# Value-row gathers four pairs behind expert-row gathers in a streaming encoder step with product-key experts

## The reference, cut to what matters

```python
def one_block(xb):                       # up to 128 tokens
    q = (xb @ w_q).reshape(PEER_BLOCK, P_HEADS, 2, P_HALF)
    s = jnp.einsum('nhpe,hpke->nhpk', q, subkeys)
    top_s, top_i = lax.top_k(s, P_TOPK)  # 16 of 128 keys, in each half
    ...                                  # 256 sums, the best 16 per head: idx, (tokens, 8, 16)
    g = jax.nn.softmax(best_s, axis=-1)
    ue = u[idx]                          # rows of 1024 floats
    ve = v[idx]
    a = jax.nn.gelu(jnp.einsum('nd,nhkd->nhk', xb, ue))
    return jnp.einsum('nhk,nhkd->nd', g * a, ve)
```

## Time and profile before

| what | value |
|---|---|
| time, median of 3 runs | 4091.41 us (4071.89 to 4091.5) |
| span of the profiled execution | 4095.0 us |
| PE busy | 2611.7 us (64%) |
| DVE busy | 2381.8 us (58%) |
| POOL busy | 2496.3 us (61%) |
| DMA, mean over the span | 361 GB/s, 1478.18 MB |
| u and v gathers | 1152 and 1152, of 512 KB |
| first dot of stage 1 | 590.6 us after the span's start |

### The profile page before, as it was taken

How to read it: one execution, slowest core, us unless ns; L and a number is a source line. 1 busy time by engine, 2 the same in 40 slices (tenths; PEclk the granted TensorE clock), 3 DMA queues, 4 the chain that set the end, 5 groups by cost and what they waited for, 6 DMA issues and landing times.

```text
span 4095.0 us, 31715 instructions
## 1 busy us (share of the span) xinstructions
PE 2611.7 (64%) x9649; PEld 951.6 (23%) x9649; DVE 2381.8 (58%) x6038; ACT 459.4 (11%) x1098; POOL 2496.3 (61%) x2374
## 2 busy tenths in 40 slices
PE   7878664654564465546456675665555687767789
PEld 2344341221231111212112132222212221111122
DVE  2247687875666456645764565776566657754410
ACT  2234220111010000100010011011001100000000
POOL 1102446667777667665765565566667677777776
PEclk8889876777776686768677787867777799999999
DMA  8855888999999999989998998999899999999999
GB/s 340 304 182 162 303 275 301 353 343 360 371 397 372 364 409 384 383 335 407 405 400 326 400 391 305 389 380 355 337 409 407 361 403 409 405 410 409 409 409 374
DMA packets 480551, 1478.18 MB, mean 361 GB/s; under 512 B 59088, under 2 KB 132864, under 8 KB 479712
## 3 DMA queue, kind: packets, MB, share of 16 engines
q0 software_dynamic: 347792, 1268.25, 80.6%
q1 hardware_dynamic: 107008, 195.85, 13.1%
q10 hardware_dynamic: 25584, 12.06, 1.0%
HBM read 1448.97 MB, written 28.57 MB: 361 GB/s over the span
## 4 chain that ended last, share of the span: by engine, by line
DMA 36%; POOL 22%; PE 18%; DVE 13%; issue 9%; ACT 1%; SPq 0%; ACTq 0%; DVEq 0%; POOLq 0%
DMA A<-in_uv,A 34%; POOL A L2013 12%; POOL A L2033 10%; PE P L961 9%; DVE A L1832 6%; PE P L869 1%; PE P L687 1%; PE P L839 1%; PE P L624 1%; PE P L826 1%; DVE A L1495 1%; PE P L706 1%; PE P L853 1%; DVE A L1704 1%; DVE A L1707 1%
## 5 line engine op out<-in xcount | busy, mean ns | idle before, releaser
L961 PE MATMUL P<-A 128*32 128x512 f32 x4608 | 1323.4, 816 | 1257.4 <-DMA A<-in_uv,A 1193.5
L2013 POOL DMA_INDIRECT A<-in_uv,A x1152 | 1245.2, 1081 | 811.9 <-DVE A L1832 560.5
L1832 DVE CUSTOM_DVE_ANT_0 A<-A 128x1024 f32<-128x1024 f32 x900 | 1094.7, 1224 | 817.0 <-DMA A<-in_uv,A 809.3
L2033 POOL DMA_INDIRECT A<-in_uv,A x1152 | 1205.5, 1046 | 428.0 <-issue 312.4
L961 PEld LDWEIGHTS P<-A 128*32 128x32 f32 x4608 | 270.5, 133 | 2120.5 <-issue 1662.1
L1832 DVE CUSTOM_DVE_ANT_0 A<-P,A 128x1024 f32<-128x1024 f32 x252 | 308.3, 1224 | 268.5 <-DMA A<-in_uv,A 267.3
L978 PE MATMUL P<-A 128*128 128x512 f32 (+1 forms) x480 | 229.8, 625 | 13.5 <-DMA A<-in_w_kv 6.9
L869 PE MATMUL P<-A 128*128 128x512 f32 (+1 forms) x320 | 181.2, 694 | 6.3 <-DMA A<-in_w_oA 5.6
L839 PE MATMUL P<-A 128*128 128x128 f32 (+2 forms) x832 | 147.4, 310 | 36.2 <-DVE A L1667 35.4
L826 PE MATMUL P<-A 96*64 96x320 f32 (+9 forms) x320 | 146.5, 560 | 10.1 <-DMA A<-qA_scratch 4.7
L2041 POOL DMA_DIRECT2D A<-in_ada_w x28 | 21.3, 763 | 199.8 <-PE P L624 155.5
(11 more groups left out here) (191 smaller groups left out, 2117.7 us busy)
## 6 DMA issues: line engine op xcount, KB each, us to landing
A<-in_ada_w POOLq DMA_DIRECT2D x28, 2048.0 KB, 10.0
A<-in_w_kv SPq DMA_DIRECT2D x80, 512.0 KB, 9.0
A<-in_uv,A POOLq DMA_INDIRECT x2304, 8.2
A<-in_w_oA SPq DMA_DIRECT2D x40, 512.0 KB, 7.6
A<-in_w_q SPq DMA_DIRECT2D x40, 512.0 KB, 8.1
A<-in_w_oB SPq DMA_DIRECT2D x40, 512.0 KB, 9.0
A<-in_p_w_q SPq DMA_DIRECT2D x2, 4096.0 KB, 16.2
A<-in_p_w_q SPq DMA_DIRECT2D x8, 512.0 KB, 5.2
```

What stands on the lines that cost most here:

```text
L961: ins = pe.matmul(Y[32 * j:32 * j + 32, b, :], spread[:, w:w + STRIDE], row[:, 512 * b:512 * b + 512], start=(m == 0), stop=(m == STRIDE - ...
L1832: dve.tensor_tensor_reduce(u_slot[b], row, u_slot[b], 1.0, 0.0, ALU.mult, ALU.add, dots[u % 2][:, j:j + 1]).then_inc(sem("dots_done"), 1)
L2013: pool.indirect_dma_start(u_slot[at % U_SLOTS], None, table, bass.IndirectOffsetOnAxis(ap=expert[u % 2][:, j:j + 1], axis=0)).then_inc(sem ...
L2033: pool.indirect_dma_start(row, None, table, bass.IndirectOffsetOnAxis(ap=expertT[u % 3][:, n:n + 1], axis=0)).then_inc(sem(name), 16)
```

## The change

A constant `LAG = 4` is added. POOL's v gathers come from a generator over all units and run four places behind the u gathers, across the ends of stages too: the first four places of a stage now bring the last value rows of unit s-2. On DVE, `add_experts`, the second part of `ready`, the later parts of `between` and the `heads` pulls move later; on every engine the heads of stage 1 and of the middle stages are spread over two value steps fewer. ACT takes its heads before the exponential of the choice as 7 and 9 in place of 8 and 9.

```diff
+LAG = 4
 ...
         def pulls(stage, m):
             if stage == 1:
-                return (m - 13) * 7 // 6 - (m - 14) * 7 // 6 if m >= 14 else 0
+                return (m - 13) * 20 // 16 - (m - 14) * 20 // 16 if m >= 14 else 0
             if not has_middle(stage):
                 return 1 if m >= 8 else 0
-            return (m - 17) * 3 // 2 - (m - 18) * 3 // 2 if m >= 18 else 0
+            return (m - 17) * 20 // 12 - (m - 18) * 20 // 12 if m >= 18 else 0
...
                     else:
-                        pull(heads, 8 if stage else 4)
+                        pull(heads, 7)
                         choose_exp(*chosen_unit, 0)
-                        pull(heads, 9 if stage else 7)
+                        pull(heads, 9)
...
-                    elif j == 3 and stage >= 2:
+                    elif j == max(3, n * (LAG + 2) // EXPERTS) and stage >= 2:
                         add_experts(*place(stage - 2))
...
-                        if e in ((32, 38) if stage == 1 else (5, 9)):
+                        if e in ((32, 42) if stage == 1 else (5, 14)):
                             pull(ready)
-                        elif e in (24, 29, 32, 47, 51, 63, 66):
+                        elif e in (24, 38, 40, 51, 55, 67, 70):
                             pull(between)
...
                         if e >= 62 and e % 3 if stage == 1 else e > 30 and e % 12 in (0, 2, 5, 7, 10):
                             pull(picks)
-                        if e % 4 == 2 and e >= 6:
-                            pull(heads, pulls(stage, e // 4 - 1))
+                        if e % 4 == 2 and e >= 6 + LAG:
+                            pull(heads, pulls(stage, (e - LAG) // 4 - 1))
...
+            def value_rows():
+                for u in range(UNITS):
+                    pool.wait_ge(sem("expertsT_ready"), u + 1)
+                    if u == 0:
+                        pool.wait_ge(sem("q_multiplied"), 4 * TILES)
+                        pool.wait_ge(sem("v_multiplied"), 2 * len(KEYS_A))
+                        pool.memset(spread, 0.0).then_inc(sem("spread_zeroed"), 1)
+                    for i in range(ROWS[ORDER[u % TILES]]):
+                        gather_v(*place(u), i)
+                        yield
+            rows, late = value_rows(), [0] * LAG
             for stage in range(UNITS + 1):
...
                         gather_u(*place(stage), i)
-                    for i in range(vs * j // max(us, vs), vs * (j + 1) // max(us, vs)):
-                        if i == 0:
-                            pool.wait_ge(sem("expertsT_ready"), stage)
...
-                        gather_v(*place(stage - 1), i)
+                    late.append(vs * (j + 1) // max(us, vs) - vs * j // max(us, vs))
+                    pull(rows, late.pop(0))
+            for _ in rows:
+                pass
```

## The result

| | before | after |
|---|---|---|
| time, median of 4 runs | 4090.07 us (4071.89 to 4091.5) | 4140.99 us (4131.99 to 4150.24) |
| ratio, 95% interval | | 1.0141 (1.0113 to 1.0168) |
| span of the profiled execution | 4095.0 us | 4142.1 us |
| DVE busy | 2381.8 us | 2381.6 us |

The changed kernel is slower by 51 us, or 1.4%. Beside the second set of experiments it ran five times more, on another chip, and stood there at 1.0094 (1.0062 to 1.0126), 37 us over the kernel before. So the loss is 0.9 to 1.4%. In the new file every line after the first additions is one further on (L1841 is `list_rows`, L1704 the first search of the picks, L962 the value steps); the two gathers are L2014 (u) and L2034 (v).

What follows compares the result with a forecast made beforehand. The stream of gathers was taken to bound the kernel. 56 + 53.5 + 12 - 71 = 50 us more: a span of 4145 against 4095.0, so a median of 4141 us, 1.2% slower; range 4062 to 4190.

Steps and rivals of the forecast that it cites:

- What bounds the kernel: Whole kernel: the stream of gathers bounds it, so a change is worth what it does to the stream's holes.
- The signs that it named: Waits: L1840 for L928 7 to 10 us, L1703 for L1369 9 to 11; POOL stops move; L1694's and L1495's nearly go.
- What is taken away: Nine holes, 71 us: 41 at dot 29 in mid-stage, 20 from late heads at stage starts, 10.8 in stage 5.
- the 10.8 us of stage 5: Stage 5, POOL waiting for a v slot: four rows of slack remove the whole hole.
- `list_rows`: Starts of stages 2 to 9: DVE waits after dot 0 for value step 31's late row; adds 56 us.
- The clock run forward for stage 8: Start of stage 8: row lands after 8.05 us, dot 1 starts at 3268.0, u gather 5 comes 10.1 us late.
- The first pick: Stages 2, 3, 4, 6, 7, 8: pick stays at e = 31 while key scores come four places later; adds 53.5 us.
- Stage 1: Stage 1: `list_rows` after dot 36 and picks from e = 62 wait for later value steps; adds 12 us.
- Heads squeezed: Heads going from 14 value steps to 13: between 0 and 10 us more, taken as 0.
- That the new waits hide: Rival, chance 0.16: POOL's stops do not reach the DMA engines; 4020 us, or 4055 with half the gain given back.
- A landing as fast as the fastest, 4.3 us: Nearly-equal rival, chance 0.18: fast value rows cut 3.7 us from each of eight start waits; 4111 us.
- The Trainium skill's fixed time plus bytes: Rule weighed, not used: 2.0 us plus bytes at 436 GB/s, 3.2 us per gather; 39 us less, giving 4102.

Runs made afterwards that it cites:

- The run without a lag: Changed kernel with LAG = 0 and DVE's moved places taken back by four, kept relative to PE: 4025.33 us, 0.9838; on a slow chip 4155.03 us, 0.989.
- The two halves alone: Kernel before with only `between` parts at e = 34 and 36: 4182.51 us, 0.9943; kernel before with only heads ended by value step 29: 4182.49 us, 0.9954.
- The run with both edits: Changed kernel with picks, `list_rows` and `spread_weights` moved later, `add_experts` one dot later: 4024.1 us, 0.983; on a slow chip 4161.44 us, 0.9892.
- The run with the heads alone: Kernel before with only the heads of stages 1 and 3 to 7 ended by value step 29: 4182.49 us, 0.9954.

## Why the prediction was right

**What bounds the kernel** held. DVE did the same work in the same time, and the time followed the holes of the stream. The idle time of the stream from 590 us to the end rose by 46 us and the profiled span by 47 (51 us in the picked windows, and 51 between the medians). The signs that it named came: the waits of L1841 and L1704, POOL's stops before u gathers 5 and 35 in place of 4 and 33, and nearly the end of the waits of L1694 and L1495. Only the waits at the starts ran up to 14.5 us, where 7 to 10 were named.

**What is taken away**, 71 us. The run without a lag, which keeps just this part, gained 71 us (4096.01 to 4025.33). The agreement is partly luck, since it does not touch the 10.8 us of stage 5. The two halves alone gained 24 and 19 us on a slow chip, where 41 and 20 were forecast; both together gained 1.1% on the slow chip of the first set, against 1.6% on the second chip. If every gain shrinks so on such a chip, 41 and 20 would be 27 and 13 there, an estimate. So these two runs do not show that either half was priced wrong. That the first pick takes over some of what `between` gave up is seen in stages 3 and 6 alone.

Of stage 5, the prediction took the hole as gone. In fact 4.5 us of it stay, the window at 2187. DVE's wait for the list is there (8.87 us), but it is not what stopped POOL. POOL stood for value slots, as it did before the change, only for less long: 16.01 us before, 5.02 the longest now. The run with both edits, in which `list_rows` is moved, has the same stops. The first line is the changed kernel's, the second that run's:

```profile
2173.19 0.93 POOL L2034 DMA_INDIRECT A<-in_uv,A  x1 [5.02 <-PE P L962]
```

```profile
2145.20 0.93 POOL L2034 DMA_INDIRECT A<-in_uv,A  x1 [5.59 <-PE P L962]
```

**`list_rows`**, 56 us forecast, 63 us of holes found; without stage 5, 53 and 59. The clock run forward for stage 8 gave POOL a stop 10.1 us beyond its turn; it stood 8.97 us (the row landed in 6.7 us and not in 8.05). The terms listed there add up to 3268.3 and not 3268.0, so the stop should have read 10.4. The largest errors in POOL's stops are in stages 4 and 7. POOL stood 14.00 us in stage 4 and 13.91 in stage 7, from these timelines of the changed kernel:

```profile
1752.68 0.95 POOL L2014 DMA_INDIRECT A<-in_uv,A  x1 [0.30 <-issue]
...
1753.94 0.94 POOL L2034 DMA_INDIRECT A<-in_uv,A  x1 [0.30 <-issue]
...
1754.35 2.06 SPq L374 DMA_DIRECT2D A<-in_w_kv  x4
...
1765.69 3.64 PE L962 MATMUL P<-A 128*32 128x512 f32 x16 [10.30 <-DMA A<-in_uv,A]
...
1771.67 1.68 POOL L2014 DMA_INDIRECT A<-in_uv,A  x1 [14.00 <-DVE A L1833]
```

```profile
2845.56 1.94 SPq L374 DMA_DIRECT2D A<-in_w_kv  x4
...
2849.94 0.94 POOL L2034 DMA_INDIRECT A<-in_uv,A  x1 [0.30 <-issue]
...
2861.64 3.63 PE L962 MATMUL P<-A 128*32 128x512 f32 x8 [11.52 <-DMA A<-in_uv,A]
```

In both stages 2 MB of SP's loads began beside the last value row, and it landed 11.7 us after its issue (1753.94 and 2849.94). In stages 2, 3, 6 and 8, where no such loads run, it took 6.4 to 8.3 us. The prediction had left open whether these loads would fill the new holes or delay the last row. They did both: POOL's stop grew by 4 us and more, and yet the holes in those two windows (7.0 and 8.7 us) are hardly longer than the 8.5 of stage 8, or shorter. In stage 6 there is no load; its hole, 10.6 us where 8.6 was said, is the longest. POOL has a value row to send at every second place only there; that this is the reason was not tried.

**The first pick**, 53.5 us forecast, 45 us found. Stage 8 is right to a tenth (a wait of 8.65 us where 8.7 was said). The term that was over-sized is stage 3, 9 us forecast and 2.3 found, though POOL stood 10.27 us there: the 4 MB load, and 2 MB more, were issued in that stop, at 1433 to 1436 us, and filled nearly all of it. In stages 6 and 7 the holes were 10.2 us each, against 8 and 10.

**Stage 1**, 12 us forecast, 14 found. From its first u gather to that of stage 2 it took 13 us longer than before.

**Heads squeezed**, taken as nothing. The prediction says from 14 value steps to 13; in the middle stages the code makes it 12 (18 to 29). The run with the heads alone gained 19 us where 20 were forecast, so no cost of it is seen.

**The sum**, 50 us, was met by the first measurement (51 us) and is 13 us over the second (37 us). The terms erred by up to 8 us each and in both directions. Taken stage by stage, from a stage's first u gather to the next one's, they miss by as much or more: stage 3 grew by 4 us where its terms add up to 13, stage 5 shrank by 15 where they give 8, and what follows the start of stage 9 grew by 12 where they give 6. So the hit to a microsecond is chance; the interval of the ratio alone is 22 us wide.

**The rivals.** That the new waits hide is refuted by the windows: POOL stops of 9 us at share 0.69. A landing as fast as the fastest, 4.3 us, did not come about either. The Trainium skill's fixed time plus bytes (DMA: Bandwidth & Descriptors, "Anatomy of one DMA"), by which a gather would land in 3.2 us as an estimate, is not met in this stream: 6.7 us in stage 8 and 11.7 us in stage 4, and never under 4.8 among the changed kernel's value gathers.

## What to carry to other kernels

When a producer is set back by some places, list every wait that hangs on its last step and on each step that feeds a chain, and move all of them or none: two that were left turned a gain of 1.7% into a loss of about 1%, and leaving one of two that hang on the same step cost 28 us. Ask first whether the set-back is needed at all; here asking a few places later gained the same without it. With in-order engines and few slots the cost of such a wait can be read off the kernel before: shift the producer's rows by hand, subtract the places that the consumer has in hand, and look at which gather the blocked engine releases.

## What the runs showed of the hardware that was not expected

Chips differ in one part of the program. Two of the chips took 4203 to 4207 us for the kernel before and two took 4090 to 4096, and the last stages hold most of it. The kernel with both edits took 127 us more in the profiled execution on the first slow chip than on the second chip, and 90 of them lie behind the first u gather of stage 8. There the stream ran at 367 GB/s (share 0.96) on the first slow chip, where the chip of the result had 409 (1.03). PE also stood idle ahead of the key scores' matmuls with nothing to wait for in the profile: 14 times, 12.8 us in all, in the run without a lag on the slow chip, and not once in the same kernel on the second chip. What causes this was not tried. Gains measured there were about two thirds of those on the other chips (1.1% against 1.6% for the same kernel), so ratios from different chips are not to be set side by side to better than half a per cent.
